# The gates' product and the first decays ahead of the value projection, in a two-block fp32 transformer kernel

## The reference

```python
h = rms_norm(x, norm_mix_g[l]) * (1.0 + sc1) + sh1
proj = jnp.einsum("bsd,de->bse", h, w_in[l]) + b_in[l]
glu_in, qk_in, v, o_pre, if_pre, merge_pre = jnp.split(proj, IN_SPLITS, axis=-1)

a = glu_in[..., :CONV_WIDTH] * jax.nn.sigmoid(glu_in[..., CONV_WIDTH:])
a = causal_depthwise_conv(a, conv_dw_w[l], conv_dw_b[l])
...
qk = jax.nn.silu(causal_depthwise_conv(qk_in, qk_conv_w[l], qk_conv_b[l]))
...
log_f = jax.nn.log_sigmoid(f_pre)
...
b = jnp.cumsum(lfc, axis=-1)
d_log = jnp.where(causal, b[..., :, None] - b[..., None, :] + ic[..., None, :], -jnp.inf)
inter_log = b + m_st[..., None]
m_t = jnp.maximum(inter_log, jnp.max(d_log, axis=-1))
```

## Time and profile before

| | |
|---|---|
| median of 3 runs | 1558.11 us (1557.65 to 1559.58) |
| profiled execution | span 1558.7 us; no other time is listed for it |
| PE busy | 1535.3 us, 98% of the span |
| DVE, ACT, POOL busy | 1064.5, 715.5, 133.7 us |
| mean granted TensorE clock | 0.997 |

### The profile page before, as it was taken

How to read it: one execution, slowest core, us unless ns; L and a number is a source line. 1 busy time by engine, 2 the same in 40 slices (tenths; PEclk the granted TensorE clock), 3 DMA queues, 4 the chain that set the end, 5 groups by cost and what they waited for, 6 DMA issues and landing times.

```text
span 1558.7 us, 19501 instructions
## 1 busy us (share of the span) xinstructions
PE 1535.3 (98%) x7464; PEld 1270.6 (82%) x7464; DVE 1064.5 (68%) x1657; ACT 715.5 (46%) x1069; POOL 133.7 (9%) x131
## 2 busy tenths in 40 slices
PE   8999899999999999999999999999999999999998
PEld 3788677877888899998888787878888888888877
DVE  8998898898888799995753456766476444432356
ACT  5543578764543656653333325446354322222233
POOL 0111000000000111110021011100201101000000
PEclk9999999999999999999999999999999999999999
DMA  9778222233666546657333323111332222323331
GB/s 367 183 187 206 69 94 61 75 95 93 210 238 203 163 127 158 157 148 253 98 110 101 108 85 109 55 41 41 115 132 99 95 95 95 108 86 101 98 135 68
DMA packets 59709, 197.18 MB, mean 127 GB/s; under 512 B 7005, under 2 KB 9309, under 8 KB 59234
## 3 DMA queue, kind: packets, MB, share of 16 engines
q1 hardware_dynamic: 52208, 175.49, 34.3%
q0 software_dynamic: 7408, 20.46, 6.6%
q10 hardware_dynamic: 2, 0.00, 0.0%
HBM read 171.80 MB, written 6.30 MB: 114 GB/s over the span
## 4 chain that ended last, share of the span: by engine, by line
PE 89%; DVE 7%; ACT 2%; issue 1%; DMA 1%; ACTq 0%; POOL 0%; DVEq 0%; POOLq 0%
PE bank L1822 22%; PE bank L1814 22%; PE bank L1815 22%; PE bank L1852 3%; PE bank L1844 3%; PE bank L1843 3%; DVE convout L2430 2%; PE bank L1870 2%; DVE tmp L2501 1%; PE bank L1882 1%; PE bank L1884 1%; PE bank L1883 1%; PE bank L1957 1%; PE bank L1974 1%; DVE spl L2376 1%
## 5 line engine op out<-in xcount | busy, mean ns | idle before, releaser
L1814 PE MATMUL bank<-HH,sph 128*128 128x512 f32 x1192 | 475.7, 399 | 6.9 <-DVE spl L2376 4.7
L1815 PE MATMUL bank<-HH,spl 128*128 128x512 f32 x1192 | 466.0, 391 | 0.0
L2376 DVE TENSOR_TENSOR spl<-raw,sph 128x1024 fp32r<-128x1024 f32 (+1 forms) x206 | 259.8, 1263 | 225.0 <-ACT sph L2032 224.9
L2032 ACT ACTIVATE sph<-raw 128x1024 fp32r<-128x1024 f32 (+1 forms) x227 | 233.0, 1029 | 176.6 <-PE bank L1822 139.5
L1822 PE MATMUL bank<-HL,sph 128*128 128x512 f32 x1192 | 309.7, 394 | 0.0
L1814 PEld LDWEIGHTS bank<-HH,sph 128*128 128x128 f32 x1192 | 225.0, 189 | 58.9 <-issue 10.2
L1815 PEld LDWEIGHTS bank<-HH,spl 128*128 128x128 f32 x1192 | 224.9, 189 | 47.8 <-issue 1.5
L1822 PEld LDWEIGHTS bank<-HL,sph 128*128 128x128 f32 x1192 | 222.7, 188 | 48.6 <-issue 2.4
L2430 DVE SCALAR_TENSOR_TENSOR convout<-convin,vecs,convout 128x512 f32<-128x512 f32 x240 | 165.3, 748 | 0.0
L1814 PE MATMUL bank<-midh,sph 128*128 128x512 f32 x352 | 136.9, 389 | 0.0
L1815 PE MATMUL bank<-midh,spl 128*128 128x512 f32 x352 | 136.9, 389 | 0.0
(11 more groups left out here) (362 smaller groups left out, 2281.0 us busy)
## 6 DMA issues: line engine op xcount, KB each, us to landing
raw<-in_w_in SPq DMA_DIRECT2D x69, 512.0 KB, 3.6
raw<-in_w_up SPq DMA_DIRECT2D x66, 512.0 KB, 3.5
more<-in_w_ada SPq DMA_DIRECT2D x32, 512.0 KB, 5.0
raw<-in_w_down SPq DMA_DIRECT2D x32, 512.0 KB, 3.5
raw<-in_w_gate SPq DMA_DIRECT2D x22, 512.0 KB, 3.2
spl<-raw POOLq DMA_DIRECT2D x18, 512.0 KB, 6.0
ada<-in_w_ada SPq DMA_DIRECT2D x16, 512.0 KB, 10.9
raw<-in_w_down SPq DMA_DIRECT2D x16, 384.0 KB, 3.1
```

Of the source, the lines that this page charges most:

```text
L1814: e.matmul(P_[b][:], sph(n)[:, q], hi[:, k, :], start=k == 0, stop=False)
L1815: e.matmul(P_[b][:], spl(n)[:, q], hi[:, k, :], start=False, stop=False)
L2032: e.activation(sph(n), raw(n), ACT.Copy).then_inc(*up("s_w_high", ("wh", n)))
L2376: e.tensor_tensor(spl(n), raw(n), sph(n).bitcast(F32), ALU.subtract).then_inc(*up("s_w_low", ("wl", n)))
```

## The change

The gates' product, with what takes it out of its bank, and the registration of `decays()` now stand ahead of the two blocks of the value projection. The gates' unit has number 16 and the value units 17 to 24, where the value units had 16 to 23 and the gates' unit 24. `BY_DMA` is changed with it, so that the eight value units still get their low halves by adding transfers and the gates' unit doesn't: 18 adding transfers before, 18 after. Two main banks are lent after the value projection, as before, which is now also after the gates' product.

```diff
--- before.py
+++ after.py
@@ -42,7 +42,7 @@
 
 GMIX, GFFN = 0, 72
 
-BY_DMA = (*range(6, 24),)
+BY_DMA = (*range(6, 16), *range(17, 25),)
 
 WHOLE = (0, 1, 2, 3,)
 
@@ -608,12 +608,6 @@
     fence("v")
     add("v_begin")
 
-    for blk in range(2):
-        def evac(t, b, g):
-            add("v", blk, t, b, g)
-            return [("v", blk, t)]
-        gemm_tok("w_v", blk, 8, "n1", evac)
-
     def gates(b, g):
         j, free = tmp.take()
         k, free2 = tmp.take()
@@ -625,7 +619,6 @@
 
     forget = []
     gemm_halves("w_if", "n1", gates)
-    misc.free += [main.take() for _ in range(LENT)]
     cb, gd, mus = keepc(40), keepc(16), keepc(8)
 
     def decays():
@@ -652,6 +645,14 @@
         misc.give(b, ("cb",), ("gd",))
 
     side.append(decays())
+
+    for blk in range(2):
+        def evac(t, b, g):
+            add("v", blk, t, b, g)
+            return [("v", blk, t)]
+        gemm_tok("w_v", blk, 8, "n1", evac)
+
+    misc.free += [main.take() for _ in range(LENT)]
 
 
     fence("qk")
```

## The result

The changed kernel is slower by a third of a per cent: 1564.38 us at the median of 6 runs (1562.69 to 1565.78), the kernel before 1558.47 us beside it (6 runs, 1557.65 to 1559.58). The ratio is 1.0035, with a 95% interval of 1.0023 to 1.0046: +5.9 us by the medians and +5.5 by the ratio, between 3.6 and 7.2. The forecast was 1562.4, in a range of 1558.0 to 1566.5. The profiled execution took 1563.79 us for a span of 1561.9. All lines stand one number higher than before (L2448 was L2447).

The account below looks back on a forecast made before the run. PE, busy for 1535.3 of 1558.7 us, was taken to bound the kernel. The terms 12.0 - 6.6 - 2.1 + 1.0 gave +4.3 us, set on the median of 1558.11: 1562.4 us, range 1558.0 to 1566.5.

Parts of the forecast that it names:

- The main chain: DVE's work to the first value and through block two: unit 25 at 170.2, +12.0 us; units 25 to 29, -6.6.
- PE's side of the boundary: Between the value blocks: PE wants the first value's bank at 139.5, gets it at 145.8, a wait of 6.3 us.
- The wait for unit 18's transfer: At unit 18's low half: PE waits 2.9 us instead of 0.9, swallowed by the wait at the block boundary.
- such losses: Behind the block boundary: a clock penalty of up to 4 us would be hidden, as DVE is last at unit 25.
- The first attention: Unit 29 to the first attention: the 1.2 us wait goes and 0.95 us of decays' transposes fill a wait, -2.1 us.
- The third head: Unit 45's cut stands behind ACT's scaling: its low half comes at 309.5, PE wants it at 308.5, +1.0 us.
- New waits between 220 and 300: Sign in the changed profile that the forecast is wrong: new waits of PE between 220 and 300.
- rival (c): More late waits in the heads as attention steps move: 1 to 2 us each, 1565 to 1567 us; chance 0.13.
- 0.6 apart; set on the median: Profiled span 1558.7 and runs' median 1558.11 lie 0.6 apart; set on the median, the forecast is 1562.4 us.
- (a): DVE's reserve suffices at the block boundary: unit 25 at 160.8, +2.6 instead of +12.0, whole 1553.0 us; chance 0.07.
- (b): Memset not held up, third head doesn't wait: 2.8 us less at the boundary, 1.0 behind, 1558.6 us; chance 0.17.
- (d): ACT's gate instructions cost more in their new place, a gap behind each table load: 1565.2 us; chance 0.03.

Follow-up runs that it names:

- e3: The changed kernel with POOL's two memsets of the decays issued ahead of the gates' product: 1562.99 us, ratio 1.0026 to the kernel before.
- e1: The changed kernel with the decays back behind the value projection, their steps and the attention's at the old units: 1556.02 us, ratio 0.9980 to the kernel before.
- e7: The changed kernel with the decays registered between the two value blocks instead of ahead of both: 1567.25 us, ratio 1.0053 to the kernel before.
- e11: e1 with low halves of units 18 and 20 by DVE, fewer taps in the value stage, more in the third head: 1552.01 us, ratio 0.9959.
- e4: The changed kernel with four empty steps ahead of the first attention, putting attention at its old places: 1561.59 us, ratio 1.0016 to the kernel before.
- e12: e1 with the first attention three steps earlier and the decays' columns left in place: 1558.79 us, ratio 0.9994 to the kernel before.
- e10: The changed kernel with no taps at the gates' product, memsets early and attention at its old places: 1557.41 us, ratio 0.9989 to the kernel before.
- e5: e1 with the low half of unit 18 made by DVE instead of an adding transfer: 1555.86 us, ratio 0.9980 to the kernel before.
- e9: e1 without the nine taps at the gates' product, which go to units 33 to 36: 1557.84 us, ratio 0.9989 to the kernel before.
- e2: The changed kernel without the nine taps at the gates' product, which go to units 25 to 28: 1561.09 us, ratio 1.0018 to the kernel before.

## Why the forecast held, and where it was off

**The main chain** was right link by link. First decay at 128.0, measured 128.22; first value at 145.2, measured 145.24; unit 25 at 170.2, measured 170.18; units 25 to 29 in 22.1, measured 21.90. That the clock times agree to 0.2 us is in part luck: this profile began the taps 0.57 us late (112.01 for 111.44), and the chain from there to the first value was shorter by as much, 33.2 us for 33.8. The 1.6 us for hand-over, issue and memsets, for which no row of before stood, measured 1.35 (ACT's cut of unit 20 ended at 126.87, the first decay began at 128.22). e3 shows that the memset's wait was worth its 2.8 us on DVE, e1 that without decays the chain has 5.26 us to spare, e7 that the second block has none.

**PE's side of the boundary** was off. The forecast had PE at the bank at 139.5 and a wait of 6.3 us; it came near 141.6 and waited 4.37. The wait for unit 18's transfer (2.37, forecast 2.9) brought a stretch at the lower clock, about nine matmuls at 0.427 us instead of 0.227 from 122.02 on, 1.7 us, which I priced at the boundary only. It cost nothing in the end, as the text said of such losses: DVE was last. e11, without that wait and where DVE is not last, starts unit 25 5.4 us before e1.

**The first attention** gained 3.0 us (5.16 to 2.2), not 2.1. The step failed by taking the decays' transposes at their own 0.95 us. Before, unit 30 with the transposes in it took 6.73 us (192.55 to 199.28), 1.3 more than a unit, and unit 29 was still 0.2 longer than one; with 1.2 for the wait that makes 2.7. The last 0.3 may be the restart behind that wait, which no run separates.

**The third head**, "+1.0 us", is the term that was mis-sized: 2.5 us. The wait that it named came, at 310.00, 1.03 us long. But two more of the same kind came with it, 0.28 at 250.59 and 0.61 at 282.50, each with a restart. New waits between 220 and 300 were named as a sign of being wrong, and on this point the forecast was wrong. That is rival (c), at a part of its price. e4 takes them all out for 2.5 us in the profile and e12 puts them in for 2.2 to 2.8; the lateness of the value stage has nothing to do with them.

**The level.** The step "0.6 apart; set on the median" failed. An execution takes longer than its span: by 1.8 to 1.9 us in the changed kernel, and by 2.1 to 2.2 us in the executions of the kernel before that stand beside the experiments. With 2.1 the profiled execution of before took about 1560.8 us, above the six that stand beside the changed kernel (1559.58 at most): it held the 1.7 us stretch at 1025. I took an execution that was slower than usual for a usual one, and could not see it, as no time was listed for it.

**The sum.** Between the profiles the terms were +12.0 (0.6 of it older than the change), -6.8, -3.0, +2.5 and +0.2 up to the wait near 1025: 4.9, where the forecast had 12.0 - 6.6 - 2.1 + 1.0 = 4.3. The first attention gained 0.9 more and the third head lost 1.5 more than forecast, so the sum looks closer than its terms by luck. The last 1.0 us, to the 5.9 of the medians, lies within the interval and isn't explained.

**The rivals.** (a), the reserve suffices: unit 25 came at 170.18 and not at 160.8. Its 160.8 was too early by the forecast's own terms, since it left out DVE's second block: a first value at 139.5 and 24.3 us behind it give 163.8. e10 had no wait at the boundary and unit 25 at 164.91, and it shows that even without its three side costs the move wins no more than e1. (b): the memset was held up (e3). (d): the gates' seven instructions took 6.02 us, 118.68 to 124.70. ACT's first table load and the instruction behind it:

```profile
120.83 1.28 ACT L2079 ACT_TABLE_LOAD   x1
122.13 0.63 ACT L2079 ACTIVATE tmp<-tmp 4x512 f32<-4x512 f32 x1
```

The second begins 0.02 us behind the end of the first, as in the earlier trace rows. The drain that the Trainium skill gives ("ScalarE: Activation LUTs", "What ACT_TABLE_LOAD costs") is not in this trace either; the measurement decides.

## What to carry to other kernels

Work that is moved out of a stage where it makes a wait must be held against the spare time of the engine that does it, over all of the stage that it goes to. Here the engine had 4.9 us to spare in the first block and 0.65 in the second, and e7 showed that the second decides. Ask of each such move what comes along unasked (nine taps, a place in POOL's queue, an attention three steps earlier): here taking these three back won 7.0 us (e10), though e1, which keeps the nine taps and takes the decays back, is 1.4 us faster still. And when a wait goes, the next late thing shows: unit 20 behind unit 18 (e5), the second block behind the first (e3).

## What I had not expected of the hardware

Whether PE's clock falls behind a wait was not decided by the wait's length alone. At the same place, unit 18's transfer, eleven profiles show waits of 2.37 to 2.79 us; in nine the granted clock was 0.84 over 119 to 130, and in two (e7 with 2.55 us, e9 with 2.74) it was 1.00. Behind the 1.4 us wait near 1025 it fell in one profile of fourteen; behind the 2.25 us in e5 it didn't fall, and in e2 it fell behind the 1.81 us at unit 25 and not behind the 2.10 us at the boundary. A fall cost some 1.7 us (in e1 unit 18 took 7.10 us, 121.92 to 129.02, where a unit takes 5.44) and up to 2.9 in e3, which is as much as the terms in dispute, so a single profile of this kernel can be off by that much at each wait of this kind. The Trainium skill ("TensorE: Matmul & The Clock Gate", "What's actually happening") ties the gate to how busy the engine has been, on a count that doesn't start with the kernel; that the same wait falls out both ways agrees with it, and no run here tests it.
